# Expert outputs scaled by gates and added to the residual rows by accumulating transfers, one row per token in the last stage

## What is computed

```python
gate = g_w * top_p / jnp.sum(top_p, axis=-1, keepdims=True)        # two gates per token
expert = (g_idx * EXPERTS_PER_GROUP + top_i).astype(jnp.int32)
...
def expert_block(args):                                            # 128 rows of one expert
    xb, e = args
    hdn = jax.nn.silu(xb @ w1[e]) * (xb @ w3[e])
    return hdn @ w2[e]
...
y_assign = ybuf[dest] * sw[:, None].astype(ybuf.dtype)             # row times its gate
y = jax.ops.segment_sum(y_assign, stok, num_segments=n_tok)        # two rows per token
...
x = x + hier_moe(rmsnorm(x, norm2_g), ...)
return rmsnorm(x, final_norm_g)
```

## Time and profile before

| | us |
|---|---|
| three runs: median | 2868.65 |
| lowest and highest | 2858.72 and 2873.9 |
| the profiled execution | 2869.07 |
| its span, first to last instruction | 2867.1 |
| TensorE, VectorE, ScalarE, GpSimd busy in it | 2438.4, 1670.7, 886.7, 927.1 |

### The profile page before, as it was taken

One profiled execution on the slowest core, in us unless ns is written; L12 is line 12 of the kernel. 1 busy time (PEld: TensorE's weight loads), 2 busy tenths in 40 slices (PEclk: granted clock), 3 DMA queues, 4 the chain that ended last, 5 costly groups with the idle time before them and its releaser, 6 DMA issues. The chain is left out here.

```text
span 2867.1 us, 42766 instructions
## 1 busy us (share of the span) xinstructions
PE 2438.4 (85%) x14678; PEld 2160.5 (75%) x14679; DVE 1670.7 (58%) x1877; ACT 886.7 (31%) x2014; POOL 927.1 (32%) x686
## 2 busy tenths in 40 slices
PE   7899999888989698887999559879989999999930
PEld 6898998887979588886888447668778888777720
DVE  5532337555662255555333486995695668868736
ACT  4333322213212355564333112222222222222224
POOL 2011021221120343442222044444434445435344
PEclk9999999998989899998999769989999999999965
DMA  4112112112211466654444147965675667667559
GB/s 129 53 64 83 60 48 69 59 42 76 60 37 60 117 154 145 147 147 135 147 146 146 59 176 276 380 254 201 224 295 193 230 227 286 222 233 264 219 198 358
DMA packets 352777, 460.21 MB, mean 161 GB/s; under 512 B 115133, under 2 KB 228773, under 8 KB 352550
## 3 DMA queue, kind: packets, MB, share of 16 engines
q1 hardware_dynamic: 331700, 375.80, 39.9%
q0 software_dynamic: 13328, 55.06, 5.3%
q10 hardware_dynamic: 7634, 27.79, 2.4%
HBM read 369.25 MB, written 96.65 MB: 162 GB/s over the span
## 5 line engine op out<-in xcount | busy, mean ns | idle before, releaser
L440 PE MATMUL mix_proj<-mix_hT_high,mix_w_high 128*128 128x388 f32 (+2 forms) x1344 | 478.1, 356 | 6.5 <-ACT mix_raw L574 3.8
L440 PE MATMUL mix_proj<-mix_hT_low,mix_w_high 128*128 128x388 f32 (+2 forms) x1344 | 462.8, 344 | 0.0
L440 PE MATMUL mix_proj<-mix_hT_high,mix_w_low 128*128 128x388 f32 (+2 forms) x1344 | 461.7, 344 | 0.0
L1748 DVE TENSOR_TENSOR experts_w_low<-experts_w_whole,experts_w_high 128x2048 fp32r<-128x2048 f32 x128 | 365.4, 2855 | 4.4
L1842 PE MATMUL experts_h<-experts_w_high,experts_xT_high 128*128 x848 | 340.8, 402 | 20.8 <-DVE experts_w_low L1748 12.8
L1842 PE MATMUL experts_h<-experts_w_low,experts_xT_high 128*128 x848 | 339.2, 400 | 0.0
L1842 PE MATMUL experts_h<-experts_w_high,experts_xT_low 128*128 x848 | 337.7, 398 | 0.0
L1746 DVE CAST experts_w_high<-experts_w_whole 128x2048 fp32r<-128x2048 f32 x128 | 187.3, 1464 | 171.4 <-DMA experts_w_whole<-in_w_dram 171.3
L440 PEld LDWEIGHTS mix_proj<-mix_hT_high,mix_w_high 128*128 128x128 f32 x1344 | 261.2, 194 | 11.8 <-issue 4.8
L440 PEld LDWEIGHTS mix_proj<-mix_hT_low,mix_w_high 128*128 128x128 f32 x1344 | 261.0, 194 | 4.2 <-issue 1.8
L440 PEld LDWEIGHTS mix_proj<-mix_hT_high,mix_w_low 128*128 128x128 f32 x1344 | 260.0, 193 | 0.0
(11 more groups left out here) (306 smaller groups left out, 4698.9 us busy)
## 6 DMA issues: line engine op xcount, KB each, us to landing
experts_w_whole<-in_w_dram SPq DMA_DIRECT2D x128, 1024.0 KB, 11.6
experts_w_whole<-in_w_dram SPq DMA_DIRECT2D x32, 2048.0 KB, 18.1
delta_qkv<-feat SPq DMA_DIRECT2D x36, 768.0 KB, 7.3
y_rows<-experts_yout ACTq DMA_DIRECT2D x53, 512.0 KB
feat<-mix_out SPq DMA_DIRECT2D x100, 192.0 KB, 1.9
mix_w_whole<-in_w_tiles_dram SPq DMA_DIRECT2D x28, 512.0 KB, 3.5
normalise_x<-in_x_dram SPq DMA_DIRECT2D x18, 512.0 KB, 3.6
delta_ub<-rows SPq DMA_DIRECT2D x36, 256.0 KB, 4.6
```

What stands on the lines that cost most here:

```text
L440: m = pe.matmul(dst, w[:, kt, :], h[:, kt, lo:hi], start=kt == 0 and i == 0, stop=kt == KD - 1 and i == 2)
L1748: m = dve.tensor_tensor(low, loaded, high.bitcast(F32), ALU.subtract)
```

## The change

Each expert's output rows are multiplied by their gates as they leave PSUM, and are added to `x2_rows` in DRAM by an indirect transfer that accumulates. The last stage then reads one row for each token and normalises it.

- In the output stage, `x2_rows` and `xn_rows` get 128 rows more, for empty slots; SyncE fills them with two copies from the input and waits for these before its loop.
- The routing stage also places the gates: VectorE splits each gate in a high and a low part and multiplies `hot_block` by each, so that the 18 products per choice have 4 x 69 columns. An empty slot is recognised by a negative number (tile numbers are counted from 1) and sent to one of the extra rows, a different one for each partition. The result is the list `to` and the gates by slot, `slot_gate`.
- In the expert stage, GpSimd copies the block's gates (`block_gate`), ScalarE's output copies take them as a scale, and GpSimd adds `yo` to the rows that the list names. ScalarE no longer stores, the copies for unused blocks are gone, and the first use of `yo` is released by an extra gather into it.
- The last stage is unrolled, with six buffers; its loads are on SyncE and its stores on ScalarE, and gathers and multiply-adds are gone.

```diff
@@ -1307,6 +1307,9 @@
                 sp.dma_start(dst, src).then_inc(const, 16)
             for i in range(KD):
                 sp.dma_start(wo[:, i, :], dram["w_o"][i * P:(i + 1) * P, :]).then_inc(wo_in[i], 16)
+            for rows in (x2_rows, xn_rows):
+                sp.dma_start(rows[T:T + P, :], dram["x"][0:P, :]).then_inc(dumped, 16)
+            sp.wait_ge(dumped, 32)
...
-def route(nc, k, lg, gate, slot, table, idx):
+def route(nc, k, lg, table, to, slot_gate):
...
-        marks = [b.sb(f"marks{c}", [P, NT, 2, MAXB + 2], F32R) for c in range(2)]
+        marks = [b.sb(f"marks{c}", [P, NT, 4, MAXB + 2], F32R) for c in range(2)]
...
-        idp = b.ps("slot_tokens", [P, 2, MAXB + 2])
+        idp = b.ps("slot_tokens", [P, 4, MAXB + 2])
...
             for c in range(2):
                 pe.wait_ge(hot_set, 2 * c + 2)
                 pe.wait_ge(hot_blocks_set, 2 * c + 2)
+                pe.wait_ge(gate_marks_set, 2 * c + 2)
                 for t in range(NT):
                     m = pe.matmul(idp[:, :, :], hot_row[c][:, t, :], marks[c][:, t, :, :], start=c + t == 0, stop=c == 1 and t == NT - 1)
...
+            link(dve.tensor_copy(gate_high[:, :, :], gate[:, :, :]))
+            link(dve.tensor_tensor(gate_low[:, :, :], gate[:, :, :], gate_high[:, :, :].bitcast(F32), ALU.subtract))
...
 
                 dve.tensor_tensor(hot_block[c][:, :, :], bcast(itb[:, :], NT, 1), bcast(blk[c][:, :], MAXB + 2, 2), ALU.is_equal).then_inc(hot_set, 1)
                 dve.tensor_tensor(hot_row[c][:, :, :], bcast(itr[:, :], NT, 1), bcast(row[c][:, :], P, 2), ALU.is_equal).then_inc(hot_set, 1)
+                dve.wait_ge(hot_set, 2 * c + 1)
+                for i, part in enumerate((gate_high, gate_low)):
+                    dve.tensor_tensor(marks[c][:, :, 2 + i, :], hot_block[c][:, :, :], bcast(part[:, c, :].bitcast(F32), MAXB + 2, 2),
+                                      ALU.mult).then_inc(gate_marks_set, 1)
...
             dve.wait_ge(placed, 1)
-            link(dve.tensor_copy(marked[:, :], idp[:, 0, :]))
+            link(dve.tensor_scalar(marked[:, :], idp[:, 0, :], -float(P), None, ALU.add))
             link(dve.scalar_tensor_tensor(out=marked[:, :], in0=idp[:, 1, :], scalar=float(P), in1=marked[:, :], op0=ALU.mult, op1=ALU.add))
-            dve.tensor_copy(idx[:, :], marked[:, :])
...
+            link(dve.tensor_scalar(empty[:, :], marked[:, :], 0.0, None, ALU.is_lt))
+            link(dve.scalar_tensor_tensor(out=marked[:, :], in0=empty[:, :], scalar=dump[:, :], in1=marked[:, :], op0=ALU.mult, op1=ALU.add))
+            link(dve.tensor_copy(to[:, :], marked[:, :]))
+            link(dve.tensor_copy(slot_gate[:, :], idp[:, 2, :]))
+            dve.tensor_tensor(slot_gate[:, :], idp[:, 3, :], slot_gate[:, :], ALU.add)
...
-def experts(nc, k, dram, table, idx, xn_rows, y_rows):
+def experts(nc, k, dram, table, to, slot_gate, xn_rows, x2_rows):
...
         @block.gpsimd
         def _(pool):
             def gather(p, blk):
-                pool.tensor_copy(ix[p][:, :], idx[:, bass.ds(blk, 1)]).then_inc(e["ix_set"], 1)
+                pool.tensor_copy(ix[p][:, :], to[:, bass.ds(blk, 1)]).then_inc(e["ix_set"], 1)
 
...
+
+            def scatter(blk):
+
+                pool.wait_ge(y_added, blk * 16 + 16)
+                pool.tensor_copy(tx[:, :], to[:, bass.ds(blk, 1)]).then_inc(e["tx_set"], 1)
+                pool.wait_ge(e["tx_set"], blk + 1)
+                pool.wait_ge(e["y_set"], blk + 1)
+                pool.sem_inc(e["scatters_begun"], 1)
+                pool.indirect_dma_start(out=x2_rows[:, :], out_offset=bass.IndirectOffsetOnAxis(ap=tx[:, 0:1], axis=0),
+                                        in_=yo[:, :], in_offset=None, compute_op=ALU.add).then_inc(y_added, 16)
...
+                if not (isinstance(blk, int) and blk == 0):
+                    pool.tensor_copy(block_gate[:, :], slot_gate[:, bass.ds(blk - 1, 1)])
                 pool.wait_ge(e["silu_set"], blk + 1)
                 pool.wait_ge(e["h3_set"], blk + 1)
                 pool.tensor_tensor(s[:, :], h3, s[:, :], ALU.mult).then_inc(e["gated_set"], 1)
-
-            def empty_rows(j):
-
-
-                with pool.If(j * -2 + (2 * PAIRS - 1) >= n):
-                    dst = y_rows[bass.ds(j * (-2 * P) + (2 * PAIRS - 1) * P, 2 * P), :]
-                    pool.dma_start(dst, xn_rows[0:2 * P, :]).then_inc(emptied, 16)
-                    pool.wait_ge(emptied, j * 16 + 16)
-
-                pool.sem_inc(e["pairs_through"], 1)
+                if not (isinstance(blk, int) and blk == 0):
+                    scatter(blk - 1)
...
+            pool.indirect_dma_start(out=yo[:, :], out_offset=None, in_=xn_rows[:, :],
+                                    in_offset=bass.IndirectOffsetOnAxis(ap=ix[0][:, 0:1], axis=0)).then_inc(y_added, 16)
...
-            through_blocks(pool, n, step, empty_rows)
-            gated_low(n // 2 * 2)
+            through_blocks(pool, n, step)
+            last = n // 2 * 2
+            gated_low(last)
+            pool.tensor_copy(block_gate[:, :], slot_gate[:, bass.ds(last, 1)]).then_inc(e["last_gate_set"], 1)
+            scatter(last)
+            pool.wait_ge(y_added, n // 2 * 32 + 32)
+            pool.sem_inc(e["all_added"], 1)
...
             def output(blk):
 
-                act.wait_ge(y_free, blk * 16 + 16)
+                act.wait_ge(y_added, blk * 16 + 16)
                 for c in range(2):
 
                     act.wait_ge(e["done" if c else "y_ready"], blk + (1 + c))
-                    m = act.activation(yo[:, c * 512:(c + 1) * 512], Y[c][:, :], ACT.Copy)
+                    m = act.activation(yo[:, c * 512:(c + 1) * 512], Y[c][:, :], ACT.Copy, scale=block_gate[:, :])
                 m.then_inc(e["y_set"], 1)
-                act.wait_ge(e["y_set"], blk + 1)
-                act.dma_start(y_rows[bass.ds(blk * P, P), :], yo[:, :]).then_inc(y_free, 16)
...
-                act.wait_ge(y_free, 16 if first else blk * 16)
+                act.wait_ge(y_added, 16 if first else blk * 16)
...
-            act.dma_start(yo[0:1, :], dram["final_norm_g"].rearrange("(a n) -> a n", a=1)).then_inc(y_free, 16)
...
-            act.wait_ge(e["gated_set"], n // 2 * 2 + 1)
+            act.wait_ge(e["last_gate_set"], 1)
             output(n // 2 * 2)
...
-            act.wait_ge(y_free, n // 2 * 32 + 32)
-            act.sem_inc(e["all_stored"], 1)
...
-def combine(nc, k, dram, gate, slot, x2_rows, y_rows, y):
+
+def combine(nc, k, dram, x2_rows, y):
...
-        U = 3
+        U = 6
...
-        ix, x, out = ring("cix", [P, 2], I32), ring("cx", [P, D]), ring("out", [P, D])
-        r = [ring(f"crow{c}", [P, D]) for c in range(2)]
+        x, out = ring("cx", [P, D]), ring("out", [P, D])
...
         @block.sync
...
+            for t in range(NT):
+                if t >= U:
+                    sp.wait_ge(e["out_set"], t - U + 1)
+                sp.dma_start(x[t % U][:, :], x2_rows[t * P:(t + 1) * P, :]).then_inc(x_ld[t % U], 16)
+                if t == 0:
+                    sp.dma_start(gf[:, :], dram["final_norm_g"].partition_broadcast(P)).then_inc(const, 16)
...
         @block.vector
...
-            def sums(p, j, t):
-                dve.wait_ge(x_ld[p], j * 16 + 16)
-                dve.wait_ge(r_ld[p], j * 32 + 32)
-                g = [gate[:, c, bass.ds(t, 1)] for c in range(2)]
-                dve.scalar_tensor_tensor(out=x[p][:, :], in0=r[0][p][:, :], scalar=g[0], in1=x[p][:, :],
-                                         op0=ALU.mult, op1=ALU.add).then_inc(e["sum1"], 1)
-                dve.wait_ge(e["sum1"], t + 1)
-                dve.scalar_tensor_tensor(out=x[p][:, :], in0=r[1][p][:, :], scalar=g[1], in1=x[p][:, :],
-                                         op0=ALU.mult, op1=ALU.add).then_inc(e["sum2"], 1)
-
...
+            dve.wait_ge(const, 16)
+            for t in range(NT):
+                p = t % U
                 dve.wait_ge(e["rooted"], t + 1)
                 dve.reciprocal(ri[p][:, :], rt[p][:, :]).then_inc(e["inverted"], 1)
                 dve.wait_ge(e["inverted"], t + 1)
-                if not first:
-
-                    dve.wait_ge(stored[p], j * 16)
+                if t >= U:
+                    dve.wait_ge(stored[p], t // U * 16)
                 dve.scalar_tensor_tensor(out=out[p][:, :], in0=x[p][:, :], scalar=ri[p][:, :], in1=gf[:, :],
                                          op0=ALU.mult, op1=ALU.mult).then_inc(e["out_set"], 1)
...
         @block.scalar
         def _(act):
-            def step(p, j, t):
...
+            def store(t):
+                act.wait_ge(e["out_set"], t + 1)
+                act.dma_start(y[t * P:(t + 1) * P, :], out[t % U][:, :]).then_inc(stored[t % U], 16)
+
+            for t in range(NT):
+                p = t % U
+                act.wait_ge(x_ld[p], t // U * 16 + 16)
                 act.activation(junk[:, :], x[p][:, :], ACT.Square, accum_out=ss[p][:, :]).then_inc(e["squared"], 1)
```

(12 more changed lines are left out.)

89 lines of the change are left out of this document (22 added, 67 removed).

## The result

| | before | after |
|---|---|---|
| median of four runs each, us | 2864.53 | 2827.59 |
| lowest and highest | 2858.72, 2873.90 | 2822.66, 2829.36 |
| the profiled execution, and its span | 2869.07, 2867.1 | 2827.53, 2825.6 |

The ratio is 0.9866 with a 95% interval of 0.9842 to 0.9889. The forecast was 2832; the time came out 4 us better. The terms behind it did not come out so well, and most of what follows is about that.

The account below looks back on a forecast made before the run. It took TensorE to bound the expert stage, a VectorE and GpSimd chain routing, and transfers the last stage. From 2869.07 us, -54 + 4.5 + 5 + 6.5 + 1 = -37 gave 2832; range 2810 to 2862 (its own 2815 to 2850).

Parts of the forecast that it names:

- output stage: Output stage: two added 512 KB copies and SyncE's wait for them are hidden by 23 us of cover; zero cost.
- routing: Routing stage: gate multiplications on VectorE and a pushed-back comparison cost 6.5 us, bounds 1.1 and 9.
- start of experts: Start of the expert stage: one extra gather into the output buffer beside the first weights costs 1 us.
- last stage: Last stage: limited by bytes; 19.4 MB at 391 GB/s plus exposed ends take 56.5 us of 110.5, saving 54.
- given bound of 58.5: Last stage: upper end of the predicted gain in us, with only 2 us exposed; the lower end was 46.5.
- 7 us counted as exposed: Last stage: 3 us for the first landing and some 4 us for the last tile's chain, beside the byte time.
- third rival: Last stage: paced by a tile's chain, not bytes; at 4 us a tile it saves 38, giving 2848; chance 0.08.
- End of the expert stage: From last output copy to next stage: the accumulate's landing makes 3.0 us into 7.5, a loss of 4.5 (bounds 2 to 8).
- Each block: Expert-stage blocks: scatter work fits GpSimd's free time; worst landing 10.6 us within 11 us of room, nothing on the path.
- +5: Expert stage as a whole: scatter reads, stalls and dropped clearing copies cost 5 us net, bounds -5 to 30.
- first rival: Expert stage: the accumulate lands too late, each block waits; a landing of 18 us gives 2917; chance 0.12.
- L + 4: Expert stage: a block's loop in us for landing L; against the mean block of 20.4, time is lost from L = 16.4.

Follow-up runs that it names:

- e4: Changed kernel with two more plain 512 KB loads per tile in the last stage, into buffers nobody reads; 2877.34 us in one run.
- e3: Changed kernel with three buffers instead of six in the last stage; 2838.74 us in one run.
- e9: Changed kernel with 32 unused bytes per partition, last stage's work put behind the expert stage's without a stage end, and an early square root; 2809.87 us, ratio 0.9812.
- e2: Changed kernel with scattering transfers that write without adding, so residual and expert addition are left out; 2837.12 us in one run.
- e6: Changed kernel with the seven 1 MB clearing copies put back in the expert stage, into a tensor nobody reads; 2874.53 us in one run.
- e5b: Changed kernel where GpSimd, ahead of each accumulating transfer, sends the same rows to a side tensor and waits for their landing; 3037.74 us in one run.

## Why the prediction was right, and where it was not

**The forecast of 2832 held, but its terms erred on both sides.** Against the prediction's terms the profiled executions gave: first stages +7.75 (none foreseen), output stage +0.3 (0), routing +5.5 (+6.5), start of experts and expert stage -4.4 (+6), the end of that stage +10.0 (+4.5), last stage -60.7 (-54). The misses add up to 7.75 + 0.3 - 1.0 - 10.4 + 5.5 - 6.7 = -4.5. That 13.6 us too little and 18.1 us too much nearly cancel is luck; the direction and the range rest on the last stage, which is right.

**Last stage: the mechanism right, the size too small, beyond the given bound of 58.5 (58.9 by its own terms, 110.5 - 49.6 - 2).** It is bytes (e4). The rate was taken from a stretch whose loads included gathers and had three buffers, 391 GB/s; without them it is 420, and 19.4 MB at that rate are 46.2 us, not 49.6. Of the 7 us counted as exposed 3.7 were left. The six buffers, which the prediction gave no price, are worth 10.9 us of it (e3). The third rival, a stage paced by a tile's chain, would have left 72.5 us; three buffers go part of that way, to 60.8.

**End of the expert stage: the step that failed.** The landing was within what was said (6.2 us for the last one). But the prediction counted the landing as the only thing between the stages. It did not ask what else is put behind the instruction that now waits: the drain on GpSimd's queue, which the trace of before has, hidden, from 2742.9. e9 takes away the end of the stage, and with it the wait for this drain.

**Each block: right that nothing reaches TensorE, by a smaller margin than stated.** The worst landing was to be 10.6 and is 12.3; the h3 copy was not to wait and waited in 13 blocks. Adding costs 1.5 us of landing (e2) where 1.3 was worked out from bytes, and the Trainium skill (Collectives: The Full Stack, "The bandwidth ceiling: the fold count and why AG ≠ RS ≠ AR") has the cost in the second read. The size agrees; no run takes the read and the adding apart. The other page cited, the Trainium skill (SBUF — State Buffer, "Summary: rules for kernel authors"), would have given 12.4 for the worst landing, nearer than the prediction's own. The rows agree with it on VectorE's copies: all 38 scatters that took 2.16 us or more to issue (up to 3.70) have one whole cast of the weights inside them, 1.22 us, and end 0.35 to 0.39 us after it. The other 15 took 1.59 to 1.78 us, 13 of them beside VectorE's subtractions. One of each kind:

```profile
2003.49 2.63 POOL L1814 DMA_INDIRECT x_rows<-experts_yout,experts_slots  x1 [1.15 <-ACT experts_yout L1946]
2004.54 1.22 DVE L1778 CAST experts_w_high<-experts_w_whole 128x2048 fp32r<-128x2048 f32 x1
...
2092.40 1.62 POOL L1814 DMA_INDIRECT x_rows<-experts_yout,experts_slots  x1 [4.90 <-ACT experts_yout L1946]
2092.42 2.30 DVE L1766 TENSOR_TENSOR experts_w_low<-experts_w_whole,experts_w_high 128x2048 fp32r<-128x2048 f32 x1
```

The +5 was taken from a band of -5 to +30; two profiles of the kernel before differ by 4.2 in this stage, and both of the changed one are equal to the lower. The clearing copies, the reason for the band's lower end, are worth far more than it once scatters are there (e6, 40.6 us): they and the scatter want the same free time of GpSimd, ahead of a low part that TensorE needs.

**The first rival was set against the wrong block.** Its law, L + 4, was set against the mean of 20.4 us, and the bulk of the blocks lasts 18.0. By the same law it would begin to cost at an L of 14.0 and not 16.4, an estimate that no run has tested, since e5b put a wait on GpSimd with the later landing. With a median landing of 8.2 and a worst one of 12.3 the change passed by some 5.8 and 1.7 us, and not by 8.2 and 4.1; a chance of 0.12 was set on too wide a margin. What e5b and e6 do show is a price that no term had: a landing that GpSimd itself waits for holds up TensorE.

**Routing: the sum right, its parts not.** The 6.5 was chosen within bounds and is no sum of its terms (5.8 - 2.7 + 1.1 is 4.2). VectorE's four products took 3.5 us each and not 1.45, 14.0 against 5.8. Steps that stood beside GpSimd's pairs in the kernel before paid most of that back, as they now run while GpSimd is idle: the comparison fell from 4.45 to 2.38, and two short steps, 2.24 and 2.19 us before, to 0.17 and 0.18. The end of the products and of the stage in the changed kernel, then the two short steps of before:

```profile
1675.31 3.50 DVE L1647 TENSOR_TENSOR route_marks<-route_hot_block,route_gate_low 128x1242 fp32r<-128x1242 f32 x1
1678.74 2.38 DVE L1651 TENSOR_TENSOR route_cmp<-route_itb,route_cum 128x2144 f32<-128x2144 f32 x1
...
1686.47 0.23 DVE L1667 TENSOR_TENSOR slot_gate<-route_slot_tokens,slot_gate 128x69 f32<-128x69 f32 x1
```

```profile
1653.17 2.24 DVE L1630 TENSOR_TENSOR route_slot_block<-route_slot_f,route_slot_row 128x18 f32<-128x18 f32 x1
1655.45 2.19 DVE L1631 TENSOR_SCALAR route_slot_block<-route_slot_block 128x18 f32<-128x18 f32 x1
```

VectorE has no idle time in the changed kernel between 1656.9 and the end, so the 2.73 us that it waited for TensorE before are gone too. Together, with 1.1 us of new steps at the end, 14.0 - 2.1 - 4.1 - 2.7 + 1.1 is 6.2 us, where the stage grew by 5.5. Why a product takes 3.5 us is open: the products run beside GpSimd's pairs, but the second and the fourth outlast the pair by some 1.3 us and take no less. No run took them apart.

**The output stage was right:** its two copies of 512 KB landed 11.7 and 12.4 us after their issue, under the 23 us of cover. **The first stages were left out altogether.** That a table of other size moves buffers was in the diff, and no term asked what that does.

## What to carry to other kernels

When a transfer is moved to an engine's queue, count what follows its last landing on that queue up to the end of the stage, and what the queue's free time was used for before. Ask of a shared buffer how long the fastest blocks give it, not the mean one. When an experiment slows a loop, look what the slowed engine waits for before you read a price from it: a wait put on a queue holds up everything behind it. After a change that resizes small buffers, compare the untouched stages too: where buffers lie is part of the change, and a spare buffer can put it back.

## What the runs showed of the hardware

A store of 128-byte pieces out of a buffer at a multiple of 128 bytes takes 0.46 to 0.50 us to issue on SyncE's queue, and 0.54 to 0.66 at 32 or 96 past one (medians of a line). All buffers of the stage moved together, so which of them matters, and whether 64 bytes would do, is open. The Trainium skill (DMA: Bandwidth & Descriptors, "How a descriptor splits into AXI transactions") says that a piece is fetched in transactions that start at 256-byte boundaries; by it every second piece of a shifted buffer takes two of them and none of an aligned one. The direction agrees; that it is the cause, no run shows.

The drain at the expert stage's end on GpSimd's queue took 5.3 to 10.7 us in the ten profiled executions with scatters, and ended 10.4 to 14.3 us after the last of them was issued. It does not follow the landing: 12.4 us where that landed after 3.3 us, 12.0 where after 6.2.

A scatter's issue on GpSimd's queue took 1.59 to 1.78 us, or, where a whole cast of VectorE fell into it, until 0.4 us after the end of that cast (2.16 to 3.70 us). Two short steps of VectorE took 2.2 us beside GpSimd's pair of products and 0.18 after it.

Plain loads and stores together moved 416 GB/s over 75 us and 420 over 30, against 391 with gathers among them; with three buffers the share of busy transfer engines read 0.99 at 348 GB/s, so a share near 1 is no proof that no more bytes would fit.
